# The end of gated linear attention: last gate ahead of the states, the output's input cut chunk by chunk, the third group turned at once

## The reference, cut to what matters

```
# gla_mixer, 4 heads (dk 128, dv 256)
o_intra = (mask(q_in @ k_in.T)) @ v              # within a chunk
o_inter = q_in @ state_n                         # with the state before it
state_{n+1} = state_n * decay_n + k_dec.T @ v
o = rms_norm(o, o_gain)                          # over a head's 256 values
h = h + (o * silu(g)) @ w_out                    # <- gate, output product, residual
h = h + (p[i] @ ple_proj[i]) * sigmoid(rms_norm(h, ple_norm[i]) @ ple_gate[i])
```

## Time and profile before

| | us |
|---|---|
| median of 3 runs (lowest, highest) | 2254.57 (2251.26, 2255.41) |
| the profiled execution, its own time | 2247.51 |
| its span | 2245.7 |
| TensorE busy | 2158.1 (96%) |
| VectorE busy | 1198.7 (53%) |
| ScalarE busy | 876.6 (39%) |
| GpSimd busy | 548.1 (24%) |

### The profile page before, as it was taken

One profiled execution on the slowest core, in us unless ns is written; L12 is line 12 of the kernel. 1 busy time (PEld: TensorE's weight loads), 2 busy tenths in 40 slices (PEclk: granted clock), 3 DMA queues, 4 the chain that ended last, 5 costly groups with the idle time before them and its releaser, 6 DMA issues.

```text
span 2245.7 us, 29146 instructions
## 1 busy us (share of the span) xinstructions
PE 2158.1 (96%) x11029; PEld 1828.0 (81%) x11029; DVE 1198.7 (53%) x1615; ACT 876.6 (39%) x1475; POOL 548.1 (24%) x292
## 2 busy tenths in 40 slices
PE   4999999999999899999989999999999999999997
PEld 4778888988888788998968887888888888877886
DVE  7843332452442544334254465676766667676745
ACT  2135654111012334324142234555546656555322
POOL 3222221333332213213224222211111111110520
PEclk9999999999999999999989999999999999999999
DMA  7412212111440111101131113111111111012202
GB/s 293 145 61 75 75 67 76 55 38 54 162 159 29 68 74 47 38 29 47 38 141 48 38 38 137 34 56 37 47 56 32 42 56 47 28 47 99 89 19 75
DMA packets 40422, 157.22 MB, mean 70 GB/s; under 512 B 4993, under 2 KB 5121, under 8 KB 39058
## 3 DMA queue, kind: packets, MB, share of 16 engines
q1 hardware_dynamic: 25568, 93.52, 12.1%
q10 hardware_dynamic: 14770, 62.50, 8.0%
HBM read 128.15 MB, written 21.04 MB: 66 GB/s over the span
## 4 chain that ended last, share of the span: by engine, by line
PE 86%; DVE 9%; issue 2%; ACT 2%; DMA 0%; ACTq 0%; DVEq 0%; SPq 0%
PE psG L330 23%; PE psG L332 22%; PE psG L331 22%; PE psA L2429 2%; PE psA L2410 1%; PE psA L2411 1%; PE psA L2427 1%; PE psA L2388 1%; PE psA L2426 1%; PE psA L330 1%; PE psA L332 1%; PE psA L331 1%; PE psA L2283 1%; PE psA L419 1%; DVE FDR L2728 1%
## 5 line engine op out<-in xcount | busy, mean ns | idle before, releaser
L330 PE MATMUL psG<-AH,WH 128*128 128x512 f32 x2076 | 844.0, 407 | 26.9 <-DVE AL L1035 12.2
L331 PE MATMUL psG<-AL,WH 128*128 128x512 f32 x2076 | 818.4, 394 | 0.0
L332 PE MATMUL psG<-AH,WL 128*128 128x512 f32 x2076 | 817.9, 394 | 0.0
L317 POOL TENSOR_SCALAR WH<-RAW 128x1024 fp32r<-128x1024 f32 x144 | 165.7, 1151 | 1620.6 <-PE psG L330 1140.5
L330 PEld LDWEIGHTS psG<-AH,WH 128*128 128x128 f32 x2076 | 395.1, 190 | 105.7 <-issue 16.6
L332 PEld LDWEIGHTS psG<-AH,WL 128*128 128x128 f32 x2076 | 394.3, 190 | 86.8
L331 PEld LDWEIGHTS psG<-AL,WH 128*128 128x128 f32 x2076 | 396.0, 191 | 67.6
L319 POOL TENSOR_TENSOR WL<-RAW,WH 128x1024 fp32r<-128x1024 f32 x144 | 382.5, 2656 | 12.0
L2585 ACT ACTIVATE psA<-psA,PB 128x512 f32<-128x512 f32 x192 | 106.4, 554 | 160.2 <-PE psA L2413 123.0
L2718 DVE TENSOR_TENSOR FTL<-psA,FTH 128x512 fp32r<-128x512 f32 x192 | 106.8, 556 | 112.9 <-ACT FTH L2592 109.7
L2728 DVE RECIPROCAL FDR<-psA 64x128 f32<-64x128 f32 x128 | 118.5, 941 | 33.9 <-PE psA L2429 30.9
(11 more groups left out here) (382 smaller groups left out, 3031.0 us busy)
## 6 DMA issues: line engine op xcount, KB each, us to landing
RAW<-w_tiles SPq DMA_DIRECT2D x144, 512.0 KB, 3.4
gates<-SIG ACTq DMA_DIRECT2D x16, 512.0 KB, 2.9
park<-X ACTq DMA_DIRECT2D x2, 4096.0 KB, 11.3
CB<-fox_c ACTq DMA_DIRECT2D x16, 512.0 KB, 4.3
X<-xT SPq DMA_DIRECT2D x4, 1024.0 KB, 11.6
WADA_SCALE<-w_ada SPq DMA_DIRECT2D x2, 2048.0 KB, 20.5
WADA_SHIFT<-w_ada SPq DMA_DIRECT2D x4, 1024.0 KB, 21.1
WADA_GATE<-w_ada ACTq DMA_DIRECT2D x1, 4096.0 KB, 12.3
```

The costliest lines, as they stand in the source:

```text
L317: nc.gpsimd.tensor_scalar(WH[:, i, :], RAW[:, i % RAW_SLOTS, :], 1.0, 0.0, ALU.mult, ALU.add).then_inc(w_high, 1)
L330: first = nc.tensor.matmul(out, wh, xh, start=start, stop=False)
L331: nc.tensor.matmul(out, wh, xl, start=False, stop=False)
L332: return first, nc.tensor.matmul(out, wl, xh, start=False, stop=stop)
```

## The change

Five edits, all in the last head and behind it.

1. `GLA_AHEAD_LAST` 8 to 16: all of g1's slices stand ahead of kv 0, and steps 0 and 1 have none between them. On ScalarE g1's Silu stands in step 1, ahead of the first norm, where before it stood behind it.
2. The output's input is cut one chunk a step: chunk 0 right behind g1, ahead of the first STH; chunks 1 to 5 in steps 0 to 4. Before: two in step 2, two in 3, one each in 4 and 5.
3. Chunks 6 and 7 are cut by halves: the low 512 tokens, which are groups 0 and 1, in step 6; the high 512 after the last group. `one` and `two` take their slices of chunks 6 and 7 low half first (`by_halves`); the high ones wait for `st_ready`.
4. The third group is turned right behind the last state product (`GLA_FILL_TURN_LAST[7]` 4 to 0), and three slices, not two, stand ahead of the last turn. In all, 40 slices stand ahead of the last turn and 8 behind it, as before.
5. The residual's chunks 0 and 1 are a transfer of their own ahead of chunks 2 to 6, and the first addition waits for that one alone.

```diff
+        if by_halves:
+            order = order[:2 * N_GLA_CUT] + [(h, c) for h in range(2) for c in range(N_GLA_CUT, KC)]
...
+            elif by_halves and c >= N_GLA_CUT:
+                pe.wait_ge(st_ready, GLA_HEADS * N_ST + c - N_GLA_CUT + 1)
...
-    GLA_AHEAD_LAST = 8
-    GLA_FILL_LAST = [4, 4, 0, 1, 4, 3, 4, 2]
-    GLA_FILL_TURN_LAST = {3: 2, 5: 2, 7: 4}
+    GLA_AHEAD_LAST = 16
+    GLA_FILL_LAST = [0, 0, 3, 1, 4, 3, 4, 2]
+    GLA_FILL_TURN_LAST = {3: 2, 5: 2, 7: 0}
...
-    GLA_CUT = {2: (0, 1), 3: (2, 3), 4: (4,), 5: (5,)}
+    GLA_CUT = {0: (1,), 1: (2,), 2: (3,), 3: (4,), 4: (5,)}
...
-            queue += one[:n] + two[:n] + one[n:] + two[n:]
+            queue += one[:n] + two[:n] + one[n:n + 2] + two[n:n + 2] + one[n + 2:] + two[n + 2:]
...
         if not more:
-            fill(2)
+            fill(3)
             pe_gla_turn(pe, h, 3)
...
         gate(0)
+        if not more:
+            act.wait_ge(psum_full, u["g1"] + 1)
+            act_fill(act, 4, Y[:, 0, :], (og_read, 4), 0)
         for n in range(N_ST):
...
+            if n == 1 and not more:
+                gate(1)
...
-            if n == (3 if more else 2):
+            if n == 3 and more:
                 gate(1)
...
+            if n == 6 and not more:
+                for j in range(N_GLA_CUT, KC):
+                    act.wait_ge(og_read, h * 4 + 2)
+                    nc.scalar.activation(AH[:, j, LO], Y[:, j, LO], ACT.Copy).then_inc(a_high, 1)
...
             act_early(act, 0)
+            for j in range(N_GLA_CUT, KC):
+                act.wait_ge(og_read, h * 4 + 4)
+                nc.scalar.activation(AH[:, j, HI], Y[:, j, HI], ACT.Copy).then_inc(st_high, 1)
...
+    X_EARLY = [[slice(2, 7)], [slice(0, 8, 2)]]
+    X_FIRST = slice(0, 2)
...
+        if layer == 0:
+            act.dma_start(X[:, X_FIRST, :], park[:, X_FIRST, :]).then_inc(pos_loaded, 16)
...
-            elif j == 0:
+            elif j == 0 and layer == 0:
+                dve.wait_ge(pos_loaded, 32)
+            elif j == (0 if layer else X_FIRST.stop):
```

More of the change, by code:

```diff
@@ L375, in gemm, with gemm_slices @@
             l.then_inc(psum_full, 1)
-    def gemm_slices(pe, t, u, slot, b, fill=None, begins=0, free=True):
+    def gemm_slices(pe, t, u, slot, b, fill=None, begins=0, free=True, by_halves=False):
         mark = Begin(1)
         order = [(h, c) for h in range(2) for c in range(KC)] if fill is None else [(h, c) for c in range(KC) for h in range(2)]
+        if by_halves:
+            order = order[:2 * N_GLA_CUT] + [(h, c) for h in range(2) for c in range(N_GLA_CUT, KC)]
         def cut(h, c):
@@ L1493, in pe_gla_head @@
             n = 2 * N_GLA_CUT
-            one, two = [list(gemm_slices(pe, T_GO + j, U_GO + j, (T_GO + j) % 4, (U_GO + j) % 2, 4, 14 * j)) for j in range(GLA_BEGUN)]
-            queue += one[:n] + two[:n] + one[n:] + two[n:]
+            one, two = [list(gemm_slices(pe, T_GO + j, U_GO + j, (T_GO + j) % 4, (U_GO + j) % 2, 4, 14 * j, by_halves=True)) for j in range(GLA_BEGUN)]
+            queue += one[:n] + two[:n] + one[n:n + 2] + two[n:n + 2] + one[n + 2:] + two[n + 2:]
         def fill(n):
@@ L1736, in dve_gla_head @@
                 normalise(n // 2 - 1)
+            if n == 0 and not more:
+                dve_low(4, 0, Y[:, 0, :])
             for j in GLA_CUT.get(n, ()) if not more else ():
@@ L1740, in dve_gla_head @@
                 dve_gla_out(dve, h, n // 2 - 1)
+            if n == 6 and not more:
+                for j in range(N_GLA_CUT, KC):
+                    dve.wait_ge(a_high, KC * 4 + j + 1)
+                    nc.vector.tensor_tensor(AL[:, j, LO], Y[:, j, LO], AH[:, j, LO].bitcast(F32), ALU.subtract).then_inc(a_ready, 1)
         dve_gla_out(dve, h, 2)
@@ L1744, in dve_gla_head @@
             dve_gla_out(dve, h, 3)
-    X_EARLY = [[slice(0, 7)], [slice(0, 8, 2)]]
+            for j in range(N_GLA_CUT, KC):
+                dve.wait_ge(st_high, GLA_HEADS * N_ST + j - N_GLA_CUT + 1)
+                nc.vector.tensor_tensor(AL[:, j, HI], Y[:, j, HI], AH[:, j, HI].bitcast(F32), ALU.subtract).then_inc(st_ready, 1)
+    X_EARLY = [[slice(2, 7)], [slice(0, 8, 2)]]
+    X_FIRST = slice(0, 2)
     X_LATE = [slice(7, 8), slice(1, 8, 2)]
     def act_early(act, layer):
+        if layer == 0:
+            act.dma_start(X[:, X_FIRST, :], park[:, X_FIRST, :]).then_inc(pos_loaded, 16)
         for cs in X_EARLY[layer]:
@@ L1758, in act_mixer_out @@
             act_fill(act, f, Y[:, j, :], y_ready(j), j)
-            if j == KC - 1 and layer == 0:
-                late = X_LATE[layer]
-                act.dma_start(X[:, late, :], park[:, late, :]).then_inc(x_late, 16)
+        if layer == 0:
+            late = X_LATE[layer]
+            act.dma_start(X[:, late, :], park[:, late, :]).then_inc(x_late, 16)
         for j in range(KC):
@@ L2833, in _ @@
         act_gla(act)
-        act_mixer_out(act, 0, 4, U_GO, 3, lambda j: (og_read, 4 * (j // 2) + 4), N_GLA_CUT)
+        act_mixer_out(act, 0, 4, U_GO, 3, lambda j: (og_read, 4 * (j // 2) + 4), KC)
         act_ple(act, 0, U_PLE0, 4, 1)
@@ L2848, in _ @@
         dve_gla(dve)
-        dve_mixer_out(dve, 0, 4, U_GO, 3, N_GLA_CUT)
+        dve_mixer_out(dve, 0, 4, U_GO, 3, KC)
         dve_ple(dve, 0, U_PLE0, 4, 1)
```

## The result

The changed kernel takes 2239.11 us (median of 5, 2236.39 to 2239.73); the kernel before, now with 5 runs, 2251.5 (2247.11 to 2255.41). The ratio is 0.9941, interval 0.993 to 0.9952: 10.8 to 15.8 us less.

A forecast was written before the change was run, and what follows sets the result against it. TensorE is busy 96%, so only its stops and slow clock can be won. 12.1 less 0.3 and 2.0 is 9.8, less 0.9 clock, plus 0.5: 9.4 off 2254.6 gives 2245.2 us; range 2240.8 to 2250.5.

The forecast's parts named there:

- The work on TensorE: From g0's end to the last eight slices: unchanged work of 36.5 us; before, 14.1 more of stops and clock.
- the first rival: States' steps cost more: slow clock 1.7 after kv 4's stop, AL 4 2.2 longer; gain 5.8, 2248.8 us, chance 0.15.
- The states' steps: Kv and chunk cuts: 5.8 us stop gone, smaller stops for STF and AL, 4.3 with refills; last eight slices at 1149.1.
- The last turns: Around turns 2 and 3: no stop left, 3.3 us stop and 2.4 of slow clock gone; 12.1 gained at the eight's end.
- The cover of 0.1 us: Behind the last turn: low-half slices cover 3.08 us, the high half of chunk 6 is ready after 2.9 to 3.0.
- The residual: Additions of X behind the output product: tile 2 starts 0.2 us late; losses 0.3 there and 2.0 ahead of tile 3.
- The stop ahead of tile 3: TensorE waits there because PH waits for PST's transfer: 1.9 us, plus 0.1 of refill.
- the 1.3 for the weight load: SyncE's 512 KB weight load meets PST's transfer and takes 1.3 us from it, included in full in the stop.
- The clock, 0.9 for the stop ahead of tile 3: Slow clock behind that 1.9 us stop might cost 1.2 to 1.8; half taken, 0.9 with the longer end.
- The 0.5 by which the walk was late for the kernel before: The same walk done for the kernel before ended 0.5 us late, so 0.5 was added to the gain.
- smoother than walked: Rival: VectorE and TensorE interleave better, three stops vanish, PST lands unhindered; gain 13.8, 2240.8 us, chance 0.07.
- five stops in the steps: TensorE's stops at kv 2 (0.4), kv 4 (1.4) and for AL 3, 4, 5 (0.8, 0.5, 0.6): 3.8 us unrounded.

The follow-up runs named there:

- e6: Changed kernel with VectorE's AL 1 moved from step 0 to step 1, behind the third state update; 2239.99 us, ratio 0.995 to the kernel before.
- c3: Changed kernel with the mark that starts GpSimd's weight split at the twelfth slice of `one`, in step 5; 2240.1 us, ratio 0.9947 to the kernel before.
- e3: Changed kernel with part 3 undone: chunks 6 and 7 cut whole behind the last group; 2245.1 us, ratio 0.9966 to the kernel before.
- e4: Changed kernel with part 4 undone: third turn late again, two slices ahead of the last turn; 2237.2 us, ratio 0.9934 to the kernel before.
- e2: Changed kernel with part 5 undone: X's chunks 0 to 6 one transfer again; 2243.15 us, ratio 0.9964 to the kernel before.
- e7: Changed kernel with GpSimd's split mark moved from the first slice of `one` to its thirteenth; 2239.67 us, ratio 0.9953 to the kernel before.
- e1: The changed kernel run again, unaltered, against the kernel before; 2239.71 us, ratio 0.9945.
- e5: Changed kernel with PST loaded ahead of X's chunks 2 to 6; 2237.05 us, ratio 0.9937 to the kernel before.
- e8: Changed kernel with PST ahead of chunks 2 to 6, AL 1 behind the third state update, split mark at the thirteenth slice; 2238.9 us, ratio 0.9949.

## Why the prediction was off

The time was forecast at 2245.2 and came at 2239.1: 6.1 lower, in two halves.

**The starting point, 3.1.** I took the 9.4 off 2254.57, a median of three. With five runs the kernel before has 2251.5, with 23 others 2252.87; they scatter from 2247 to 2257. The spread of the three (2251.3 to 2255.4) did not show it, but the profiled execution at 2247.51 did, and I noted its 7 us and passed on. From 2251.5 the forecast would have been 2242.1.

**The gain, 9.4 against 12.0 in the stage.** By its own steps:

- *The work on TensorE, 36.5 us, and 14.1 of stops and clock before*: 1.6 too low, and 1.6 too high. From the end of g0's 16 slices (10.9 us) to the last eight slices the changed kernel takes 40.1, in which TensorE is idle for 2.0: 38.1 of work. The slices take 0.9 more than at 0.2275 a matmul, since the first behind a turn or a state product is some 0.1 longer (0.50 in place of 0.40), the updates and state products 0.6, the rest 0.3. With the same 38.1 the kernel before had 12.5 to win in its 50.6: 10.3 of idle and 2.2 of clock behind the first stop (the 1.7 that the first rival calls "as above" stands in no sum). What was to go went: the first stop, the last one, and with them the slow clock, 1.00 throughout.
- *The states' steps*: kv 4's stop, forecast 1.4, was 1.02, released by STF; the ones for AL, forecast 0.8, 0.5 and 0.6, were 0.28 and 0.42. The reason was right (e6, c3: VectorE is late, GpSimd's split makes it later), the term mis-sized: 4.3 with refills against 2.0 by the profile's idle. These 2.3 too many and the 1.6 of work too few leave the eight slices only 0.7 earlier than forecast. That the start of the eight came out so near is luck: two errors took each other away.
- *The last turns*: right. The cover of 0.1 us held, and e3 shows what it covers. That the third turn matters was only implied; e4 shows that it does not.
- *The residual*: the split transfer right (e2, 6.3 for the 6.6 that the same steps give). The stop ahead of tile 3 was forecast at 1.9 and was 0.30. **This is the step that failed**, in two terms. X's load went out 1.0 earlier than I had it, 0.7 of it from the terms above. And the 1.3 for the weight load did not come, which was to take its share from PST at once: PST landed 13.6 after X's first issue, as it would alone (0.4 and 13.1). The weight load was issued at 1158.52, 10.3 behind X's first issue, and its queue, q1, moved nothing from 1159.5 to 1160.5, while ScalarE's queue, q10, filled the DMA engines (queue: packets, MB, share of 16 engines):

```profile
q10 hardware_dynamic: 103, 0.42, 102.4%
```

Its first packets moved at 1161.9, 3.4 us behind the issue, when PST was in, and from 1161.8 to 1163.5 it had most of the engines:

```profile
q1 hardware_dynamic: 145, 0.55, 81.7%
q10 hardware_dynamic: 53, 0.15, 22.4%
```

It is a late start and not a place behind all of the other queue. In e7, where the load was issued 6.1 behind X's first issue, at 1153.96, its first packets moved 3.3 behind that, 5.5 ahead of PST's landing, and both queues moved from 1157 to 1159:

```profile
q10 hardware_dynamic: 70, 0.48, 57.7%
q1 hardware_dynamic: 63, 0.26, 31.8%
```

There PST did lose 1.4, near the 1.3 that I had put. The same 3.3 to 3.4 us from issue to first packet are in the profiles of e1, e5, e6 and e8, while the load at 1130.85 of the changed kernel, with no other transfer beside it, had its first packet after 1.0. The forecast had both queues share from the start. By the Trainium skill, page "DMA: Bandwidth & Descriptors", section "Queues, rings and completion order", the engines take turns packet by packet. These traces agree once both queues move: 63 packets to 70 above, 16 to 18 in e8 from 1156 to 1157, where q10's were of 20 KB and q1's of 4, so that q1 got 0.07 MB to 0.37. What they add is the 3.4 us ahead of that; why a load starts so late beside a busy queue stays open.
- *The clock, 0.9 for the stop ahead of tile 3*: that stop was too short to matter, and no slow clock followed.
- *The 0.5 by which the walk was late for the kernel before*: the walk was late for the changed kernel too, by the 0.7, so the 0.5 makes up for most of that.

0.7 + 1.5 + 0.9 less the 0.5 already in make the 2.6 that were missing. The rival "smoother than walked" (gain 13.8) was nearer than the forecast in mechanism: PST was unhindered and no clock was lost. But not three of the five stops in the steps vanished, only one; the other four were there, each shorter than forecast.

What stays open is the rest between the stage's 12.0 and the times' 12.4 to 13.2, which is within their interval. Slow clock outside the stage goes both ways between executions: at 1380 to 1385 the changed kernel had 0.66, at 1390 to 1395 the kernel before had 0.50 in one profile and 0.74 in the other. It makes up what the profiles differ by outside the stage, but which executions get it I could not tell from them.

## What to carry to other kernels

When several engines feed one, the place of a stop is not its cause: moving the work that stands just ahead of a stop (AL 1) moved the stop and won nothing; taking a block off the engine that was late (GpSimd's split) won 1.1 us and ended the two stops behind it. Parts of an edit have to be priced with each other: the transfer's split would be worth nothing without the halves, and is worth 6.3 us of the stage with them. Two errors of one sum can hide each other: the parts of a walk are to be checked and not its end alone. And a forecast of some 10 us needs the scatter of the kernel before, which three runs do not give; where the profiled execution lies far from the median, the base is part of the error.

## What the runs showed of the hardware

A stop of 3.31 us on TensorE was followed by a mean clock of 0.68 in the kernel before (7.9 us window), 0.77 in a second profile of it (7.5), 0.72 with parts 1 and 2 alone (6.0), and 1.00 in the kernel without halves. The 24 matmuls behind the stop took 7.9, 7.2, 7.2 and 5.6 us, where 5.5 are due at full clock: the same stop with a loss of 2.4, 1.7, 1.7 and 0.1. One of 1.77 (e7, e8) was followed by slow clock both times (0.70), one of 1.02 at kv 4 never in the nine profiles that have it.

VectorE's subtraction with both inputs in SBUF did not run beside GpSimd's split: 3.40 and 2.20 us for a 1.22 us operation, 2.85 for one of 0.69. In each case it ended about its own length behind GpSimd's WL (1.1 us, 1.1 and 0.55).

Beside a busy ScalarE queue, the first packet of a weight load moved 3.3 to 3.4 us behind its issue in six profiles, against 1.0 without other transfers.
